# Running sums of the Mamba decays made once a layer as rows, and their differences taken by VectorE, in a hybrid mLSTM and Mamba-2 decoder trunk

## The chip, the cores and the metric

The kernel runs on 1 core of one Trainium2 chip. The metric is the device time of one execution in microseconds. The runs shown are medians; a profiled execution gives the span, which runs from its first to its last instruction.

## The reference

Two layers of a decoder trunk on 256 tokens of width 1024, all in float32: a half-step SwiGLU, a mixer with an mLSTM branch and a Mamba-2 branch, a second half-step SwiGLU, and a gated per-layer input embedding. The change concerns the Mamba-2 branch. It has 32 heads of width 64 in 4 groups, a state of 128, and chunks of 128 tokens, so two chunks. What matters of it:

```python
acs = jnp.cumsum((dt * a_neg).reshape(bsz, nc, L, ng, ne), axis=2)      # running sums of the decays
ah = jnp.transpose(acs, (0, 1, 3, 4, 2))
decay = jnp.exp(jnp.where(causal, ah[..., :, None] - ah[..., None, :], -jnp.inf))
cb = jnp.einsum('bctgn,bcsgn->bcgts', cc, bc)
y_intra = jnp.einsum('bcgts,bcgets,bcsgep->bctgep', cb, decay, xw)
w_end = jnp.exp(ah[..., -1:] - ah)                                     # state handed to chunk 1
y_inter = jnp.einsum('bctgn,bcgepn->bctgep', cc, s_start) * jnp.exp(acs)[..., None]
```

For each head and chunk a 128x128 matrix exp(acs[t] - acs[s]) for t >= s is wanted, and for chunk 1 also exp(acs[t], from the chunk's start).

## The kernel before

**Precision.** A float32 operand x is split into x_hi (rounded to the matmul's fast type) and x_lo = x - x_hi. A projection is three matmuls: hi by hi, hi by lo, lo by hi.

**Stages.** A layer is an FFN, the mixer (a loop over 4 groups, the second to fourth in a hardware loop), the second gate, the merge of the branches, the output projection, a second FFN and the embedding gate. A weight tile (a unit, 1 MB) goes through a ring of three buffers: SyncE loads it, ScalarE writes w_hi (`hi`, L524), VectorE writes w_lo (`lo`, L911), and TensorE uses it in 48 matmuls of 256 columns (L1521). In the mixer `step(p)` on both engines means: make the copy of the unit that comes two places after place p, counted from 0. Every engine has its order written out by hand and waits on semaphores.

**One group's units on TensorE.** In groups 1 to 3: BC, QK, X01, X23, V, Z0, Z1, O, GA; in group 0 V comes first. `feat(..., between=f)` runs f in the middle of a unit (or, with place=0, after its first half). Between the units stand the products of the mixer. `cb` multiplies C by B into bank 5, `scores` makes the mLSTM's scores, `chunk_heads` (L1776) applies them and needs btok, a copy that ScalarE makes after VectorE's `mask_cb`. `inputs_transposed` (L1786) gives VectorE the inputs in token order, `state` (L1798) needs xwe from VectorE, and `outputs` (L1809) needs the decays times cb.

**Decays.** For each head, ScalarE makes R = tri_le scaled by the head's decay column, hi and lo (`part_of`, L637, one 128x128 instruction per head and part). TensorE's `segments(c, half)` multiplies tri_gt by R of four heads (two matmuls of 512 columns, L1744 and L1745) and gets acs[t] - acs[s] above the diagonal and 0 below; ScalarE's `decay(c)` exponentiates (L667). `from_start` does the same with a matrix of ones for chunk 1 (L1751, L1752), and `decay_from_start` exponentiates it into cs (L677). R of chunk 0 for the next group is built late in the group before; R of chunk 1 is built between the two exponentials of `decay(0)`.

**VectorE in groups 1 to 3, in order.** Evacuate BC; convolution of BC (`conv(0)`, L1146 and L1149); queries and keys; `step(1)`; `silu(0)` (L1160), which needs ScalarE's `tanh_conv(0)` (L662); `step(2)`; `distances` (L1176); `step(3)`; evacuate X01; `conv(1)`; `silu(1)`; `weigh_scores` (L1188), which needs GpSimd's masked exponential of `score_exp`; evacuate X23; `conv(2)`; `silu(2)`; `mask_cb` (L1182); `step(4)`; evacuate Z0; `step(5)`; weighted inputs (L1207, L1211); the gates, `step(6)`, `step(7)`, the heads' norm, `step(8)`, the outputs (L1337 to L1354) and `step(9)`.

**ScalarE in groups 1 to 3, in order.** `step(1)`, `decay(0)`, `tanh_conv(0)`, `step(2)`, `step(3)`, `decay(1)`, `tanh_conv(1)`, `score_exp`, `step(4)`, and so on. In group 0 the order is `decay(0)`, the token columns, `step(5)`, `decay(1)`, `tanh_conv(0)`, `score_exp`, `decay_from_start`, `step(6)`, `tanh_conv(1)`.

Of the kernel before, what the change touches and what calls it, by code (L numbers as in the profile page):

```python
# [5 lines left out]
F32 = mybir.dt.float32  # L6
# [6 lines left out]
P = 128  # L13
# [10 lines left out]
def trunk(nc, T, out):  # L24
# [53 lines left out]
    with ctx:  # L78
# [25 lines left out]
        tri_gt_r = sb("tri_gt_r", [P, P], F32R)  # L104
        dA_hi = sb("dA_hi", [P, NC, SH], F32R)
# [6 lines left out]
        top[0] = place(feat_at, 512, 1024)  # L112
        ha_hi = sb("ha_hi", [P, 2 * MH, S], F32R)
        ha_lo = sb("ha_lo", [P, 2 * MH, S], F32R)
        top[0] = place(top[0], 512, 1024)
# [5 lines left out]
        m_lo = sb("m_lo", [P, KD, S], F32R)  # L121
        y_feat = sb("y_feat", [P, SI // P, S])
# [9 lines left out]
        ones_r = sb("ones_r", [P, P], F32R)  # L132
# [13 lines left out]
        dA_lo = sb("dA_lo", [P, NC, SH], F32R)  # L146
# [40 lines left out]
        xwe_at = late + NC * EH * HP * 4  # L187
# [10 lines left out]
        zth_at = a  # L198
        zth, a = at("zth", [P, 2, S], F32, a)
        R_hi = [at(f"R_hi{b}", [P, 4, P], F32R, off)[0] for b, off in enumerate((xwe_at, zth_at))]  # L200
        R_lo = [at(f"R_lo{b}", [P, 4, P], F32R, late + b * 4 * P * 4)[0] for b in range(2)]
# [62 lines left out]
        def rows(x):  # L264
# [4 lines left out]
        names = """up0_done h1T_done res_done uT_done gate_done y_out_ready rB_ready z_tanh o_tanh gate_tanh evac v_ready par_ready rdiag_ready rB_done ydiag_ready yB_done yB_ready wsm_hi_ready wsm_ready pre_row_ready pre_ready acs_exp cs_ready y_done ysum_ready  # L269
# [3 lines left out]
            dA_ready dA_split ea_ready cum_done cum_exp row_tr row_ready row_back tok_ready r_built seg_done exp_done  # L273
# [133 lines left out]
        def _(pool):  # L407
# [42 lines left out]
            def group(lay, g, first, last):  # L450
# [18 lines left out]
                if not first:  # L469
                    pool.wait_ge(sem["cbm_done"], G + 1)  # L470
                    for c in range(NC):
                        pool.wait_ge(sem["exp_done"], G * 4 + (2 * c + 2))
# [3 lines left out]
                    pool.wait_ge(sem["acs_exp"], G * 2 + 2)  # L476
# [9 lines left out]
            for lay in range(DEPTH):  # L486
                row_norm(lay * 4)
                row_norm(lay * 4 + 1)
                g_.memset(M4[:, :, :], 0.0).then_inc(sem["m4_clear"], 1)
                group(lay, 0, True, False)  # L490
# [13 lines left out]
        def _(act):  # L504
# [125 lines left out]
            def groups(lay):  # L630
                def body(g, first, last):
                    G = act.snap(lay * NG + g)

                    def part_of(dst, part, g, c, half):

                        for e in range(4):
                            i = a_.activation(dst[half][:, e, :], tri_le[:, :], ACT.Copy,  # L637
                                              scale=part[:, c, bass.ds(g * EH + (4 * half + e), 1)].bitcast(F32))
                        return i

                    def distances_of(g, c, half):
                        part_of(R_hi, dA_hi, g, c, half)
                        part_of(R_lo, dA_lo, g, c, half).then_inc(sem["r_built"], 1)
# [29 lines left out]
                    def decay_from_start():  # L673

                        for b in range(2):
                            act.wait_ge(sem["seg_done"], G * 6 + (5 + b))
                            a_.activation(cs[:, 4 * b:4 * b + 4, :], bank[6 + b][:, :].rearrange("p (e t) -> p e t", e=4),  # L677
                                          ACT.Exp).then_inc(sem["acs_exp"], 1)
# [11 lines left out]
                    if first:  # L690
# [13 lines left out]
                        act.wait_ge(sem["dA_split"], lay + 1)  # L704
# [4 lines left out]
                        a_.activation(w_end[:, :], bank[7][:, 0:SH], ACT.Exp).then_inc(sem["cum_exp"], 1)  # L709
# [6 lines left out]
                        decay(0)  # L716
# [13 lines left out]
                    else:  # L730
# [9 lines left out]
                        decay_from_start()  # L740
# [49 lines left out]
                    if not last:  # L790
                        act.wait_ge(sem["yi_done"], G + 1)
                        act.wait_ge(sem["zth_ready"], G * 2 + 2)
                        for half in range(2):
                            part_of(R_hi, dA_hi, g + 1, 0, half)
                        act.wait_ge(sem["y_done"], G + 1)
                        for half in range(2):
                            part_of(R_lo, dA_lo, g + 1, 0, half).then_inc(sem["r_built"], 1)
# [1219 lines left out]
```

## Time and profile before

| | us |
|---|---|
| median of 3 runs (1563.87 to 1566.05) | 1564.98 |
| the profiled execution's own time | 1564.03 |
| its span | 1562.3 |
| busy in the span: TensorE / VectorE / ScalarE / GpSimd | 1538.5 / 1073.3 / 808.3 / 150.2 |

The mixer's groups of layer 0 lie between 204 and 465 us of the span, those of layer 1 some 769 us later. In the profile PE is TensorE's matmuls, PEld its weight loads, DVE VectorE, ACT ScalarE, POOL GpSimd; L911 is line 911 of the kernel before. A timeline row has the start, the duration, the engine, line and operation, the tiles (out<-in), how many were merged (x8) and, in brackets, how long the engine had been idle and what released it. Matmuls overlap, so the distance between two starts is what one costs.

### The profile page before, as it was taken

To read this page: it belongs to the slowest core of one execution; us is meant where nothing else is said; L and a number is where in the kernel's file an instruction comes from. 1 tells how busy PE (TensorE), PEld (TensorE's weight loads), DVE (VectorE), ACT (ScalarE), POOL (GpSimd) and SP (SyncE) were. 2 spreads that over 40 slices of the span, in tenths; PEclk is the share of its full clock that TensorE was granted. 3 is DMA by queue.
4 is the path that set the end of the run, shared out by engine and by line. 5 is a ranking of instruction groups with operands and counts; after the bars stand their busy time and mean duration, and the time that the engine had idled before them with its cause. 6 is when DMAs were issued, how large, how long until landed. Compare 5 with 4: busy or idle time off the path is not lost.

```text
span 1562.3 us, 28127 instructions
## 1 busy us (share of the span) xinstructions
PE 1538.5 (98%) x11594; PEld 1439.9 (92%) x11594; DVE 1073.3 (69%) x1313; ACT 808.3 (52%) x1141; POOL 150.2 (10%) x144
## 2 busy tenths in 40 slices
PE   7999999999999999999999999999999999999997
PEld 6999999999999979999899999998999999799996
DVE  5556578889887546565665556799889865565555
ACT  6444385664655354343564435755766643543344
POOL 1000011233130000000000000113243000000000
PEclk9999999999999999999999999999999999999999
DMA  8655544456455556655565655445545456465551
GB/s 252 196 198 190 176 156 110 146 153 185 135 159 190 190 167 210 195 188 189 173 191 194 194 194 162 128 143 144 180 134 161 161 190 213 153 207 189 188 189 68
DMA packets 245089, 271.09 MB, mean 174 GB/s; under 512 B 12560, under 2 KB 226152, under 8 KB 245012
## 3 DMA queue, kind: packets, MB, share of 16 engines
q1 hardware_dynamic: 239504, 266.90, 53.7%
q10 hardware_dynamic: 5364, 2.98, 0.7%
q8 instruction: 53, 0.87, 0.2%
q14 instruction: 24, 0.20, 0.0%
q0 software_dynamic: 144, 0.15, 0.0%
HBM read 268.94 MB, written 1.05 MB: 173 GB/s over the span
## 4 chain that ended last, share of the span: by engine, by line
PE 89%; DVE 4%; issue 4%; ACT 2%; DMA 1%; SPq 0%; POOL 0%; ACTq 0%; DVEq 0%; POOLq 0%
PE bank L1521 29%; PE bank L1605 28%; PE bank L1551 8%; PE bank L1552 7%; PE bank L1553 7%; PE bank L1954 1%; PE bank L1809 1%; PE bank L1546 1%; DVE w_lo L911 1%; PE bank L1537 1%; PE bank L1539 1%; PE bank L1538 1%; ACT w_hi L524 1%; DMA w_raw<-in_w_ffn_dram 1%; DVE xcv L1149 1%
## 5 line engine op out<-in xcount | busy, mean ns | idle before, releaser
L911 DVE TENSOR_TENSOR w_lo<-w_raw,w_hi 128x2048 fp32r<-128x2048 f32 x248 | 577.0, 2328 | 315.8 <-ACT w_hi L524 315.5
L524 ACT ACTIVATE w_hi<-w_raw 128x2048 fp32r<-128x2048 f32 x248 | 474.1, 1916 | 307.5 <-PE bank L1605 131.0
L1605 PE MATMUL bank<-f_lo,w_hi 128*128 128x256 f32 x1280 | 355.7, 278 | 0.0
L1605 PE MATMUL bank<-f_hi,w_lo 128*128 128x256 f32 x1280 | 353.5, 276 | 0.0
L1605 PE MATMUL bank<-f_hi,w_hi 128*128 128x256 f32 x1240 | 342.7, 276 | 0.0
L1521 PE MATMUL bank<-u_hi,w_hi 128*128 128x256 f32 x1152 | 326.5, 283 | 1.3 <-DVE w_lo L911 1.3
L1521 PE MATMUL bank<-u_lo,w_hi 128*128 128x256 f32 x1152 | 319.8, 278 | 0.0
L1521 PE MATMUL bank<-u_hi,w_lo 128*128 128x256 f32 x1152 | 319.8, 278 | 0.0
L1605 PEld LDWEIGHTS bank<-f_hi,w_lo 128*128 128x128 f32 x1280 | 240.5, 188 | 0.0
L1605 PEld LDWEIGHTS bank<-f_lo,w_hi 128*128 128x128 f32 x1280 | 240.4, 188 | 0.0
L1605 PEld LDWEIGHTS bank<-f_hi,w_hi 128*128 128x128 f32 x1240 | 232.8, 188 | 0.0
L1521 PEld LDWEIGHTS bank<-u_hi,w_hi 128*128 128x128 f32 x1152 | 216.4, 188 | 6.3 <-issue 4.1
L1521 PEld LDWEIGHTS bank<-u_lo,w_hi 128*128 128x128 f32 x1152 | 216.7, 188 | 1.3
L1521 PEld LDWEIGHTS bank<-u_hi,w_lo 128*128 128x128 f32 x1152 | 217.2, 189 | 0.0
L1551 PE MATMUL bank<-w_hi,h_hi 128*128 128x512 f32 x352 | 137.5, 391 | 0.0
L1553 PE MATMUL bank<-w_hi,h_lo 128*128 128x512 f32 x352 | 137.2, 390 | 0.0
L1552 PE MATMUL bank<-w_lo,h_hi 128*128 128x512 f32 x352 | 137.2, 390 | 0.0
L436 POOL TENSOR_TENSOR rms<-var,m_half 128x2 f32<-128x2 f32 x11 | 7.7, 696 | 1019.9 <-DVE var L947 998.9
L584 ACT ACTIVATE sa<-h1f 128x512 f32<-128x512 f32 x40 | 25.3, 632 | 118.4 <-DVE h1f L995 118.4
L1553 PEld LDWEIGHTS bank<-w_hi,h_lo 128*128 128x128 f32 x352 | 66.1, 188 | 14.0
L1552 PEld LDWEIGHTS bank<-w_lo,h_hi 128*128 128x128 f32 x352 | 66.1, 188 | 12.3
L1551 PEld LDWEIGHTS bank<-w_hi,h_hi 128*128 128x128 f32 x352 | 66.1, 188 | 12.3
(301 smaller groups left out, 2450.8 us busy)
## 6 DMA issues: line engine op xcount, KB each, us to landing
w_raw<-in_w_ffn_dram SPq DMA_DIRECT2D x262, 512.0 KB, 4.4
w_raw<-in_w_in_dram SPq DMA_DIRECT2D x160, 512.0 KB, 4.9
w_raw<-in_w_branch_b_dram SPq DMA_DIRECT2D x32, 512.0 KB, 4.5
w_raw<-in_w_branch_a_dram SPq DMA_DIRECT2D x16, 512.0 KB, 4.5
w_raw<-in_w_out_dram SPq DMA_DIRECT2D x16, 512.0 KB, 4.0
w_raw<-in_w_ple_gate_dram SPq DMA_DIRECT2D x16, 512.0 KB, 4.4
y_feat<-in_w_ple_dram ACTq DMA_DIRECT2D x2, 1024.0 KB, 5.0
h<-in_x_dram SPq DMA_DIRECT2D x2, 512.0 KB, 5.7
```

Source lines behind the costliest of these rows:

```text
L524: a_.activation(whi[slot][:, :, :], raw[slot][:, :, :], ACT.Copy).then_inc(sem["w_hi"], 1)
L584: a_.activation(sa[:, :, :], h1f[:, :, :], ACT.Silu).then_inc(sem["g_silu"], 1)
L911: v_.tensor_tensor(wlo[slot][:, :, :], raw[slot][:, :, :], whi[slot][:, :, :].bitcast(F32), ALU.subtract).then_inc(sem["w_lo"], 1)
L1149: ins = v_.scalar_tensor_tensor(out=dst[:, q, :], in0=src, scalar=gcw[:, j, t:t + 1], in1=dst[:, q, :], op0=ALU.mult, op1=ALU.add)
L1521: i = mm(o, w[slot][:, k, cs], x[:, k, :], start=(k + q == 0 and not seeded), stop=(k == KD - 1 and q == 2 and not seeded), skip_group_che ...
L1537: mm(o, xh[:, k, cs], whi[slot][:, k, :], start=(k == 0), stop=False)
L1538: mm(o, xh[:, k, cs], wlo[slot][:, k, :], start=False, stop=False)
L1539: i = mm(o, xl[:, k, cs], whi[slot][:, k, :], start=False, stop=(k == KD - 1))
L1551: mm(o, xh, wh, start=start, stop=False, skip_group_check=True)
L1552: mm(o, xh, wl, start=False, stop=False, skip_group_check=True)
L1553: return mm(o, xl, wh, start=False, stop=stop, skip_group_check=True)
L1605: i = mm(o, four(w[slot])[:, k, cs], x[:, rows0 + k, :], start=opens, stop=(not start and k == 3 and q == 2), skip_group_check=True)
```

## The change

The decays' running sums are computed once a layer. dA is split into `twin[0]` (hi) and `twin[1]` (lo), each with its 8 heads of a group at columns 0 to 7 and again at 32 to 39. TensorE multiplies the twins by tri_le (16 matmuls of 128 columns), so the sums stand as rows 0 to 7 and 32 to 39. ScalarE rounds them into `acs`, and VectorE replaces rows 32 to 39 by the rest, so that row e plus row 32+e is the full sum. In a group one matmul per head, with a matrix `pick` that has ones in rows e and 32+e, spreads a head's sums over all partitions for both chunks (256 columns). VectorE subtracts the sum at s (`acol`, a column per head and chunk) and clamps at 0; ScalarE exponentiates. Nothing of R is left. The core of the diff (tile placement, semaphore names and unchanged lines left out):

```diff
@@ gpsimd, once a layer, ahead of group 0
+                g_.memset(acs[:, :, :].bitcast(F32), 0.0)
+                for b in range(2):
+                    i = g_.memset(twin[b][:, :, :, :].bitcast(F32), 0.0)
+                i.then_inc(sem["twin_clear"], 1)
+                for b in range(2):
...
+                    i = g_.tensor_tensor(pick[b][:, :, :], ident[:, e].unsqueeze(2).broadcast_to([P, EH // 2, P]),
+                                         ident[:, f].unsqueeze(2).broadcast_to([P, EH // 2, P]), ALU.add)
+                i.then_inc(sem["pick_ready"], 1)
@@ scalar
-                    def part_of(dst, part, g, c, half):
-                        for e in range(4):
-                            i = a_.activation(dst[half][:, e, :], tri_le[:, :], ACT.Copy,
-                                              scale=part[:, c, bass.ds(g * EH + (4 * half + e), 1)].bitcast(F32))
-                        return i
+                    def sums_high():
+                        act.wait_ge(sem["acs_done"], lay + 1)
+                        for b in range(2):
+                            i = a_.activation(acs[0:40, 2 * b:2 * b + 2, :],
+                                              bank[4 + b][0:40, :].rearrange("p (g s) -> p g s", g=2), ACT.Copy)
+                        i.then_inc(sem["acs_hi"], 1)
...
-                    def decay(c):
-                        for b in range(2):
-                            act.wait_ge(sem["seg_done"], G * 6 + (2 * c + b + 1))
-                            a_.activation(seg[:, c, 4 * b:4 * b + 4, :],
-                                          bank[4 + 2 * c + b][:, :].rearrange("p (e t) -> p e t", e=4),
-                                          ACT.Exp).then_inc(sem["exp_done"], 1)
-                            if c == 0:
-                                distances_of(g, 1, b)
...
+                    def decay(half):
+                        act.wait_ge(sem["gap_ready"], G * 2 + (half + 1))
+                        for e in range(4 * half, 4 * half + 4, 2):
+                            a_.activation(cs[:, e:e + 2, :], two(4 + e // 2)[:, :, P:2 * P], ACT.Exp)
+                        a_.activation(seg[:, :, 4 * half:4 * half + 4, :], seg[:, :, 4 * half:4 * half + 4, :],
+                                      ACT.Exp).then_inc(sem["exp_done"], 1)
@@ scalar, group 0
-                        distances_of(g, 0, 0)
-                        distances_of(g, 0, 1)
+                        sums_high()
                         step(3)
...
                         step(5)
+                        act.wait_ge(sem["cum_exp"], lay + 1)
+                        tanh_conv(0, bcv[:, :, :])
+                        decay(0)
+                        score_exp()
                         decay(1)
-                        tanh_conv(0, bcv[:, :, :])
-                        score_exp()
-                        decay_from_start()
                         step(6)
@@ vector
+                    def gaps(half):
+                        dve.wait_ge(sem["cum_exp"], lay + 1)
+                        dve.wait_ge(sem["seg_done"], G * 2 + (half + 1))
+                        for e in range(4 * half, 4 * half + 4):
+                            for c in range(NC):
+                                i = v_.tensor_scalar(seg[:, c, e, :], bank[4 + e // 2][:, (e % 2) * S + c * P:(e % 2) * S + (c + 1) * P],
+                                                     acol[:, c, bass.ds(g * EH + e, 1)], 0.0, ALU.subtract, ALU.min)
+                        i.then_inc(sem["gap_ready"], 1)
@@ vector, group 0
                         conv(1, 1, (2, 3), xcv[:, 0:2, :])
+                        gaps(0)
                         weigh_scores()
+                        evac(X23, xin[:, 0, :, 3:])
+                        gaps(1)
                         mask_cb()
-                        evac(X23, xin[:, 0, :, 3:])
                         silu(1, xcv[:, 0:2, :])
@@ vector, groups 1 to 3
                         step(1)
+                        gaps(0)
                         silu(0, bcv[:, :, :])
                         step(2)
                         distances()
                         step(3)
+                        gaps(1)
                         evac(X01, xin[:, 1, :, 3:])
@@ tensor, once a layer (in gates)
+                pe.wait_ge(sem["dA_split"], lay + 1)
+                for g in range(NG):
+                    for c in range(NC):
+                        o = bank[4 + g // 2][0:40, (g % 2) * S + c * P:(g % 2) * S + (c + 1) * P]
+                        mm(o, twin[0][:, c, g, :], tri_le_r[:, :], start=True, stop=False)
+                        i = mm(o, twin[1][:, c, g, :], tri_le_r[:, :], start=False, stop=True)
+                i.then_inc(sem["acs_done"], 1)
@@ tensor, in a group, in place of segments and from_start
+                    def sums(half):
...
+                        for e in range(4):
+                            i = mm(bank[4 + 2 * half + e // 2][:, (e % 2) * S:(e % 2 + 1) * S], pick[half][:, e, :],
+                                   acs[:, bass.ds(g, 1), :].rearrange("p a b -> p (a b)"), start=True, stop=True)
+                        i.then_inc(sem["seg_done"], 1)
```

In groups 1 to 3 `sums(0)` stands in the middle of QK and `sums(1)` in the middle of X01; in group 0 they stand after `scores` and in the middle of Z0. `cb` now waits for the first `decay`, `inputs_transposed` for the second. VectorE splits dA into the twins in two copies and two subtractions instead of one each, and `sums_low`, two subtractions on 8 partitions, follows `gate_rows` in group 0. A second product next to the one for w_end, 64 columns wide, gives `acol`, which ScalarE copies.

## Rows read from the trace of the kernel before

**Rows 1.** The page: busy time of each engine, its share of the span, instructions.

```profile
PE 1538.5 (98%) x11594; PEld 1439.9 (92%) x11594; DVE 1073.3 (69%) x1313; ACT 808.3 (52%) x1141; POOL 150.2 (10%) x144
```

**Rows 2.** Stretches; length, then busy PE, PEld, DVE, ACT, POOL; clock, DMA share, GB/s.

```profile
281.71:341.96 60.25, 58.30 (x503) 55.58 (x501) 51.95 (x72) 38.29 (x70) 19.73 (x17) 1.00 0.48 140
341.96:403.25 61.29, 61.29 (x529) 59.23 (x528) 53.09 (x74) 38.78 (x70) 19.88 (x16) 1.00 0.53 154
```

**Rows 3.** Timeline, VectorE, groups 2 and 3; start, duration, then [idle before <- releaser].

```profile
340.37 2.29 DVE L911 TENSOR_TENSOR w_lo<-w_raw,w_hi 128x2048 fp32r<-128x2048 f32 x1 [2.59 <-ACT w_hi L524]
...
343.30 0.74 DVE L1146 TENSOR_SCALAR bcv<-xin,gcw,gcb 128x256 f32<-128x256 f32 x2
...
349.57 0.68 DVE L1160 SCALAR_TENSOR_TENSOR bcv<-cth,bcv 128x512 f32<-128x512 f32 x1
350.74 2.29 DVE L911 TENSOR_TENSOR w_lo<-w_raw,w_hi 128x2048 fp32r<-128x2048 f32 x1 [0.49 <-ACT w_hi L524]
...
404.20 0.74 DVE L1146 TENSOR_SCALAR bcv<-xin,gcw,gcb 128x256 f32<-128x256 f32 x2
...
412.03 2.29 DVE L911 TENSOR_TENSOR w_lo<-w_raw,w_hi 128x2048 fp32r<-128x2048 f32 x1 [0.87 <-ACT w_hi L524]
```

**Rows 4.** Timeline, ScalarE, around and in group 2.

```profile
336.23 1.05 ACT L801 ACTIVATE zs<-y_feat 128x1024 f32 x1
...
342.62 0.60 ACT L667 ACTIVATE seg<-bank 128x512 f32<-128x512 f32 x1 [0.49 <-PE bank L1745]
...
348.28 0.61 ACT L662 ACTIVATE cth<-bcv 128x512 f32<-128x512 f32 x1
348.80 3.70 ACT L524 ACTIVATE w_hi<-w_raw 128x2048 fp32r<-128x2048 f32 x2
...
368.53 0.27 ACT L688 ACTIVATE btok<-bank 128x128 f32<-128x128 f32 x1
...
373.35 0.36 ACT L750 ACTIVATE cst<-bank 128x257 f32<-128x257 f32 x1
373.61 0.38 ACT L751 ACTIVATE num<-bank 128x257 f32<-128x257 f32 x1
```

**Rows 5.** Timeline, TensorE, groups 2 and 3.

```profile
341.96 0.39 PE L1744 MATMUL bank<-R_hi,tri_gt_r 128*128 128x512 f32 x1
...
342.42 0.28 PE L1521 MATMUL bank<-u_hi,w_hi 128*128 128x256 f32 x1
342.54 0.28 PE L1521 MATMUL bank<-u_lo,w_hi 128*128 128x256 f32 x1
...
370.06 0.59 PE L1776 MATMUL bank<-vtok,ktok 128*128 128x257 f32 x2
...
371.36 1.03 PE L1786 MATMUL bank<-ident,xcv 128*128 128x128 f32 x8
...
431.34 0.59 PE L1776 MATMUL bank<-vtok,ktok 128*128 128x257 f32 x2
```

**Rows 6.** Groups of ScalarE instructions by line: count, busy us, mean ns, idle before.

```profile
L637 ACT ACTIVATE R_hi<-tri_le,dA_hi 128x128 fp32r<-128x128 f32 x128 | 40.0, 389 | 2.1 <-DVE dA_lo L1086 2.1
```

**Rows 7.** Timeline, VectorE, a burst of eight 128x128 instructions that read PSUM.

```profile
201.76 2.15 DVE L954 SCALAR_TENSOR_TENSOR u_lo<-bank,par,u_hi 128x128 fp32r<-128x128 f32 x8
```

**Rows 8.** Timeline, VectorE and TensorE, group 0 of layer 0.

```profile
238.79 0.69 DVE L1160 SCALAR_TENSOR_TENSOR bcv<-cth,bcv 128x512 f32<-128x512 f32 x1 [5.43 <-ACT cth L662]
...
247.21 0.68 DVE L1160 SCALAR_TENSOR_TENSOR xcv<-cth,xcv 128x512 f32<-128x512 f32 x1
...
243.15 0.60 PE L1760 MATMUL bank<-bcv 128*128 128x128 f32 x4
```

**Rows 9.** Timeline, TensorE, start of the execution.

```profile
10.39 0.63 PE L1552 MATMUL bank<-w_lo,f_hi 128*128 128x512 f32 x1
10.81 0.63 PE L1553 MATMUL bank<-w_hi,f_lo 128*128 128x512 f32 x1
...
18.27 0.39 PE L1552 MATMUL bank<-w_lo,f_hi 128*128 128x512 f32 x1
```

More of the change, by code:

```diff
@@ L103, in trunk @@
         gate_a = sb("gate_a", [P, KD, S])
[L104 to L105 removed]
+        tri_le_r = sb("tri_le_r", [P, P], F32R)
+        acol = sb("acol", [P, NC, SH])
         e_a = sb("e_a", [P, SH])
@@ L112, in trunk @@
         top[0] = place(feat_at, 512, 1024)
+        ha_hi_at = top[0]
         ha_hi = sb("ha_hi", [P, 2 * MH, S], F32R)
+        ha_lo_at = top[0]
         ha_lo = sb("ha_lo", [P, 2 * MH, S], F32R)
+        last_group = 2 * (MH - 1) * S * 4
+        pick = [at(f"pick{b}", [P, EH // 2, P], F32R, off + last_group)[0] for b, off in enumerate((ha_hi_at, ha_lo_at))]
         top[0] = place(top[0], 512, 1024)
@@ L186, in trunk @@
         late = a
-        xwe_at = late + NC * EH * HP * 4
+        twin = [at(f"twin{b}", [P, NC, NG, 40], F32R, late + b * 40 * NC * NG * 4)[0] for b in range(2)]
         xw, a = at("xw", [P, NC, EH * HP], F32, a)
@@ L789, in body @@
                         step(9)
[L790 to L797, printed above, removed]
                     act.wait_ge(sem["ha32_ready"], G + 1)
@@ L1265, in body @@
                         gate_rows(lay)
+                        sums_low(lay)
                         step(3)
@@ L1739, in unit @@
                         kind((K_MIX + p) % RING, p % RING, u_hi, u_lo)
-                    def segments(c, half):
-                        pe.wait_ge(sem["r_built"], G * 4 + (2 * c + half + 1))
-                        mm(bank[4 + 2 * c + half][:, :], tri_gt_r[:, :], R_hi[half][:, :, :], start=True, stop=False)
-                        mm(bank[4 + 2 * c + half][:, :], tri_gt_r[:, :], R_lo[half][:, :, :], start=False, stop=True)\
-                            .then_inc(sem["seg_done"], 1)
-                    def from_start():
-                        for half in range(2):
-                            pe.wait_ge(sem["exp_done"], G * 4 + (3 + half))
-                            mm(bank[6 + half][:, :], ones_r[:, :], R_hi[half][:, :, :], start=True, stop=False)
-                            mm(bank[6 + half][:, :], ones_r[:, :], R_lo[half][:, :, :], start=False, stop=True)\
-                                .then_inc(sem["seg_done"], 1)
+                    def sums(half):
+                        if first:
+                            pe.wait_ge(sem["acs_ready"], lay + 1)
+                            pe.wait_ge(sem["pick_ready"], lay + 1)
+                            pe.wait_ge(sem["cum_exp"], lay + 1)
+                        elif half == 0:
+                            pe.wait_ge(sem["st_ready"], G)
+                            pe.wait_ge(sem["num1_ready"], G)
+                        else:
+                            pe.wait_ge(sem["y_ready"], G)
+                        for e in range(4):
+                            i = mm(bank[4 + 2 * half + e // 2][:, (e % 2) * S:(e % 2 + 1) * S], pick[half][:, e, :],
+                                   acs[:, bass.ds(g, 1), :].rearrange("p a b -> p (a b)"), start=True, stop=True)
+                        i.then_inc(sem["seg_done"], 1)
                     def cb():
                         pe.wait_ge(sem["cv_ready"], G * 3 + 1)
-                        pe.wait_ge(sem["exp_done"], G * 4 + 2)
+                        pe.wait_ge(sem["exp_done"], G * 2 + 1)
                         for c in range(NC):
@@ L1839, in body @@
                         pe.wait_ge(sem["tok_ready"], lay * 2 + 2)
-                        segments(1, 0)
-                        segments(1, 1)
-                        unit(Z0, lambda *a: feat(*a, between=from_start))
+                        sums(0)
+                        unit(Z0, lambda *a: feat(*a, between=lambda: sums(1)))
                         cb()
@@ L1858, in body @@
                         unit(BC, feat)
-                        unit(QK, lambda *a: feat(*a, between=lambda: segments(0, 0)))
-                        segments(0, 1)
-                        unit(X01, lambda *a: feat(*a, between=lambda: segments(1, 0)))
-                        segments(1, 1)
+                        unit(QK, lambda *a: feat(*a, between=lambda: sums(0)))
+                        unit(X01, lambda *a: feat(*a, between=lambda: sums(1)))
                         evac(QK)
@@ L1865, in body @@
                         unit(X23, feat)
-                        unit(V, lambda *a: tok(*a, between=from_start))
+                        unit(V, tok)
                         cb()
```

64 lines of the change are left out of this document (32 added, 32 removed).

## The prediction

> **What bounds the kernel now.** I read the page first: TensorE is busy 98% of the span, VectorE 69%, ScalarE 52%, GpSimd 10% [rows 1]. Nearly all TensorE time is projections that the change leaves alone, so matmuls taken away should shorten the run, if the engines that feed TensorE can follow a faster one. The share of 69% doesn't settle that. In the stretch of one group (layer 0, group 2) VectorE is busy 53.1 of 61.3 us [rows 2], against 69% of the whole, so I went through that stretch instruction by instruction.
>
> VectorE stands still 8.2 us in that group, and the question is whether any of it waits for TensorE. The timelines say that nearly none does. Its largest idle piece (2.59 us) waits for ScalarE's copy of a weight tile, which itself followed a tanh of what VectorE had just written; the others are pieces under 1 us of the same kind, such as the tanh that ScalarE can start only when VectorE's convolution ends. These are round trips that VectorE starts, and no faster TensorE shortens them. The only waiting for TensorE that reaches this loop is ScalarE's 0.49 us before its first exponential of the group, handed on as the 0.49 us that VectorE waits at 350.74 [rows 3, 4]. From group 2 to group 3 VectorE's round takes 404.20 - 343.30 = 60.9 us; without the 0.49 it takes 60.4. TensorE's round is 431.34 - 370.06 = 61.3 us [rows 5]. So two loops are within 0.9 us of each other. In group 1 VectorE's is the longer: TensorE is busy only 58.3 of 60.3 us there [rows 2]. That is the ground of the forecast: a change that takes from TensorE and gives to VectorE's round makes the kernel slower.
>
> **TensorE.** Two 512-column matmuls take from 341.96 to 342.42, 0.23 us each; a 256-column one takes 0.12 us [rows 5]. A group loses 12 of 512 (8 in `segments`, 4 in `from_start`), 2.8 us, and gains 8 of 256, 0.95 us: 1.85 us less, 14.8 us over 8 groups. Once a layer come 16 matmuls of 128 columns on the twins. The nearest row is that of eight transposes of this width, 1.03 us with a last one of 0.27, so 0.11 us from start to start [rows 5]; I take that, 1.8 us, and 0.2 us for the wider sum for `acol`; bounds 0.5 and 4 us a layer. TensorE's own sum is then 14.8 - 4.0 = 10.8 us less, if nothing makes it wait.
>
> **ScalarE.** 256 copies of 128x128 that build R go, 40 us busy for R_hi and as much for R_lo [rows 6], 32 per group. That gives nothing by itself: they fill ScalarE between 342.6 and 348.3, and what VectorE then lacks is the 0.49 us above. The others, late in a group, lie under VectorE's own work (ScalarE still waits for it after them). Six exponentials of 512 from PSUM become four of 256 (start to start 0.26 us [rows 4]) and two of 1024 from SBUF (1.05 us [rows 4]).
>
> **VectorE, groups 1 to 3.** Added are 16 `tensor_scalar` of 128x128 from PSUM. Eight of nearly this kind take 2.15 us in a burst [rows 7]: 2.1 us for each half, 4.2 us a group. Bounds for one: 0.14 us (half of the burst's 0.27) to 0.34 us (the duration of one that is not overlapped, as 8 by 0.34 instead of 2.1): 2.2 to 5.5 us a group. `gaps(0)` stands between `step(1)` and `silu(0)`, and `decay(0)` stands on ScalarE ahead of `tanh_conv(0)`. So where the tanh had long been ready (VectorE starts `silu(0)` at 349.57 without waiting, tanh from 348.28 [rows 3, 4]), this now runs in series, in times of group 2:
> - `gaps(0)` 349.57 to 351.7;
> - `decay(0)` two cs exponentials 0.26 + 0.26, then 1024 elements: the tanh starts at 353.3 and ends 353.9; VectorE has waited 2.3 us;
> - `silu(0)` 353.95 to 354.55;
> - the copy for `step(2)` follows the tanh, 353.8 to 355.7 (1.9 us, [rows 4]); VectorE waits 1.2 us more, and starts at 355.75 instead of 350.74: +5.0.
>
> `gaps(1)` then adds 2.1 us ahead of the evacuation of X01. Its ScalarE part (1.6 us) is hidden under convolution 1 (3.5 us). So `mask_cb`, `step(4)` and all behind them come 7.1 us later. The waits for nothing but round trips further down the group remain; none of them is for an engine that runs ahead, so none absorbs the delay. Group 3 had a longer wait for that copy, 0.87 us at 412.03 [rows 3]: +6.7. Group 1 has the same order and waits of its own: +7.0.
>
> TensorE has no room for this: its chunk_heads at 370.06 waits for btok, ready at 368.80 [rows 4, 5]. There it will stand: a new round is 60.4 + 7.0 = 67.4 us, against 59.4 us of TensorE work, so 8 us of waiting a group, mostly before chunk_heads and some before V's weights.
>
> **Group 0.** Walked in the same way from layer 0. ScalarE's `sums_high` waits for the sums of the twins, which TensorE ends near 225.9 (its small gate products start at 223.0) behind X01's first half, and VectorE's `sums_low` adds 1.3 us; but VectorE stood 5.43 us before `silu(0)` [rows 8] and this covers it: `silu(0)` comes at 238.0 instead of 238.79. Then: `step(4)` 239.1, conv(1) to 245.1, `gaps(0)` to 247.2. Now `weigh_scores` needs `score_exp`, which stands behind `decay(0)` (to 248.85), then 0.4 us of exp and 0.95 us on GpSimd: 250.2, 3 us idle. Evacuation of X23, `gaps(1)` to 253.3, and `silu(1)` waits for tanh(1), behind `decay(1)` (1.6) and `step(6)` (1.8) on ScalarE: 257.3 instead of 247.21 [rows 8], +10.1; 0.2 of it is lost in the wait for the transposed inputs. TensorE meets it twice: `cb`, at 243.15 before [rows 8], waits for `decay(0)` until 248.9, and chunk_heads for btok. If ScalarE could reach `step(6)` earlier, as it would with a shorter pair of exponentials, +7; if the twins' sums come later than I put them, +12.
>
> The new memsets, `pick` on GpSimd (once a layer, about 5 us) and the double split of dA (0.2 us) run at the front of the layer: GpSimd is busy a tenth of the span [rows 1], and its taps are first used by the convolution of group 0, over 10 us later. I cost them at 0; without that cover up to 2 us a layer. No DMA is added or moved.
>
> **Sum.** A layer: 9.9 + 7.0 + 7.1 + 6.7 = 30.7 us, less the room that TensorE had: between 0 and the 1.26 us from btok to chunk_heads; I take 0.6: 30.1. Behind the groups TensorE is the bound again and gives nothing back. The profiled execution took 1564.0 us; 1564.0 + 60.2 = 1624.2. The median of the runs is 0.95 us over that execution: **1625 us**. The 10.8 us that TensorE saves don't count, since they become waiting. Its own range, 2.2 to 5.5 us for the 16 instructions and 7 to 12 for group 0: 1608 to 1639.
>
> **Rivals.**
> - *Waits hidden, work not* (12%). ScalarE, without its copies, would be ready early enough that only VectorE's 4.2 us a group remain, against 0.9 us of room. For it speaks ScalarE's idle time; against it, that `decay(0)` itself starts only after `gaps(0)`. 8 x (4.2 - 0.4) = 30: 1595 us.
> - *TensorE stays the bound* (8%, the other side). If `silu(0)` and the weight splits had over 7 us of room in each group, the 10.8 us would come through, and with them up to 2 us of group 1's waits a layer (60.25 - 58.30 [rows 2]): 1550 us. The place is X23's and Z1's weights, which VectorE finishes at 349.66 and 370.4, under 2 us ahead of use by my reading of TensorE's order; it decides below 0.9 us of net delay a group. TensorE's 98% speaks for it, and rows 3 against it.
> - *The clock falls* (8%). The granted clock is 1.00 in all stretches read [rows 2], and TensorE never stands long there. At the start of the run, after standing, matmuls of 512 columns come every 0.42 us, not 0.23 (1.2 instead of 2.4 GHz), at 10.39 and still shortly before 18.27 [rows 9]. Should each long stop (one or more a group, 5 to 6 us) bring back such a stretch, its 7.9 us of half speed cost 3.9 us, of which some 1.5 lie under VectorE's lag: 8 x 2.4 = 19 us more, 1644 us. The Trainium skill (TensorE: Matmul & The Clock Gate, "HAM oscillation — how this bites in real kernels") has the mechanism: a loop in which TensorE stands waiting each turn restarts at the throttled clock. By that rule this rival would be the likeliest. No row before shows a fall in mid-run, so I leave it at 8%.
> - *No change* (3%): losses meet gains of the same size.
>
> **How the numbers follow.** Forecast 69%. Faster is the second rival, 8%; within 0.2% (3 us, what a measurement tells from none) 3%; slower 89%. The range reaches below to the waits-hidden rival and above nearly to the clock's: 1594 to 1646.
>
> **What would show it.** Right: VectorE waits about 2.3 us before `silu(0)` for ScalarE's tanh and about 1.2 us for the copy behind it; eight-bursts of 2.1 us; the round of a group 67 to 68 us in groups 1 to 3; TensorE's idle before chunk_heads, with btok as releaser, about 6 us; in group 0, `cb` waits for an exponential. Wrong: TensorE busy over 99% of the groups and a round near 59.5 us, or bursts of well under 2 us. If the granted clock falls below 1.00 within the groups, the third rival is in it.

## The result, and the profile after the change

The changed kernel takes 1625.79 us (1625.22 to 1628.05, 4 runs) against 1564.42 us (1563.60 to 1566.05, 4 runs) beside it: ratio 1.0395 [1.0383, 1.0407], slower. Its profiled execution has a span of 1624.0 us (before 1562.3).

The page's busy line, against [rows 1]: TensorE fell from 98% to 95%, and ScalarE lost 72 us of work without any gain. TensorE's busy time rose by 11.4 us though it was given less work; the mean granted clock of its execution fell from 0.998 to 0.982.

```profile
PE 1549.9 (95%) x11598; PEld 1450.3 (89%) x11598; DVE 1109.3 (68%) x1448; ACT 736.6 (45%) x891; POOL 153.2 (9%) x154
```

One round of VectorE (group 2's first convolution to group 3's) by stretches, as in [rows 2]: length, busy PE, PEld, DVE, ACT, POOL, then clock. It has grown from 60.9 to 67.9 us, TensorE is no longer busy all through it, and its clock is below 1.00.

```profile
360.33:428.26 67.93, 61.87 (x519) 59.49 (x519) 56.92 (x90) 29.42 (x37) 19.51 (x15) 0.95 0.47 139
```

VectorE's timeline in group 2, which answers to [rows 3]. Both bursts of eight and both predicted waits are there: 2.19 us before `silu(0)`, 1.11 us before `step(2)`'s w_lo.

```profile
366.59 2.15 DVE L1215 TENSOR_SCALAR seg<-bank,acol 128x128 f32<-128x128 f32 x8
370.93 0.69 DVE L1165 SCALAR_TENSOR_TENSOR bcv<-cth,bcv 128x512 f32<-128x512 f32 x1 [2.19 <-ACT cth L669]
372.73 2.29 DVE L902 TENSOR_TENSOR w_lo<-w_raw,w_hi 128x2048 fp32r<-128x2048 f32 x1 [1.11 <-ACT w_hi L534]
...
377.66 2.16 DVE L1215 TENSOR_SCALAR seg<-bank,acol 128x128 f32<-128x128 f32 x8
379.73 0.68 DVE L1140 TENSOR_TENSOR xin<-bank,rB 128x512 f32<-128x512 f32 x1
```

ScalarE beside it ([rows 4] before). It stood idle 9.61 us, then did the exponentials, the tanh and two weight copies in a row, with VectorE waiting for the third and fourth link.

```profile
368.78 0.66 ACT L675 ACTIVATE cs<-bank 128x256 f32<-128x256 f32 x2 [9.61 <-DVE seg L1215]
369.32 1.06 ACT L676 ACTIVATE seg<-seg 128x1024 f32<-128x1024 f32 x1
370.27 0.63 ACT L669 ACTIVATE cth<-bcv 128x512 f32<-128x512 f32 x1
370.79 3.72 ACT L534 ACTIVATE w_hi<-w_raw 128x2048 fp32r<-128x2048 f32 x2
```

TensorE's chunk_heads, where [rows 5] had no stop: it waits 5.83 us for btok. Behind the stop, a pair of 257-column products takes 0.85 us (393.94 to 394.79), half speed: at full clock such a pair took some 0.43 us (258.49 to 258.93 in e_order).

```profile
392.95 1.20 PE L1806 MATMUL bank<-vtok,ktok 128*128 128x257 f32 x2 [5.83 <-ACT btok L687]
393.94 1.06 PE L1807 MATMUL bank<-vtok,scT 128*128 128x257 f32 x2
394.79 1.07 PE L1808 MATMUL bank<-vtok,scT 128*128 128x257 f32 x2
```

The same place by stretches: the granted clock, 1.00 all through the groups of before [rows 2], is 0.71 in the mean after the stop and 1.00 again in the next stretch. Layer 0 has five such falls, one with each of TensorE's stops of over 2 us: one of 5.78 us ahead of cb in group 0, one of 2.56 us early in group 1, and those of 4.29, 5.83 and 5.59 us ahead of chunk_heads in groups 1 to 3.

```profile
386.00:393.00 7.00, 1.17 (x11) 1.01 (x10) 6.16 (x13) 2.75 (x7) 0.62 (x1) 0.80 0.00 0
393.00:400.00 7.00, 7.00 (x38) 6.34 (x39) 7.00 (x5) 4.63 (x5) 7.00 (x2) 0.71 0.59 151
400.00:407.00 7.00, 7.00 (x60) 6.01 (x60) 6.88 (x5) 1.91 (x1) 3.87 (x2) 1.00 0.55 148
```

Group 0 on VectorE, against [rows 8]: `silu(0)` waits 2.40 us in place of 5.43, `weigh_scores` waits for GpSimd, `silu(1)` for ScalarE.

```profile
238.94 0.69 DVE L1165 SCALAR_TENSOR_TENSOR bcv<-cth,bcv 128x512 f32<-128x512 f32 x1 [2.40 <-ACT cth L669]
...
250.59 0.42 DVE L1193 TENSOR_TENSOR scT<-pm,bank 128x256 f32<-128x256 f32 x1 [2.77 <-POOL pm L467]
...
257.67 0.69 DVE L1165 SCALAR_TENSOR_TENSOR xcv<-cth,xcv 128x512 f32<-128x512 f32 x1 [3.66 <-ACT cth L669]
```

### The profile page after: what moved, and what is told of

The parts are those of the page before. It is cut to its first block, busy times and chain, and to the rows that moved or that the text cites. A ratio compares the mean times of both kernels' runs of the same rounds, so it can differ in the third digit from the quotient of the medians.

```text
span 1624.0 us, 27967 instructions
## 1 busy us (share of the span) xinstructions
PE 1549.9 (95%) x11598; PEld 1450.3 (89%) x11598; DVE 1109.3 (68%) x1448; ACT 736.6 (45%) x891; POOL 153.2 (9%) x154
## 4 chain that ended last, share of the span: by engine, by line
PE 69%; DVE 12%; issue 10%; POOL 4%; ACT 4%; DMA 1%; DVEq 0%; SPq 0%; ACTq 0%; POOLq 0%; another core or an unknown queue 0%
PE bank L1623 26%; PE bank L1539 16%; PE bank L1569 7%; PE bank L1570 7%; PE bank L1571 7%; DVE w_lo L902 2%; POOL seg L474 2%; DVE xcv L1154 2%; ACT w_hi L534 2%; DVE seg L1215 2%; PE bank L1979 1%; PE bank L1564 1%; POOL cs L477 1%; DVE xin L1140 1%; DVE xcv L1151 1%
```

## The experiments

Theory from here on: VectorE's chain, with the round trips it makes through ScalarE, sets the length of a group; it grew by its own 4.2 us and by two waits that ScalarE's order makes. All times are medians; all ratios are to the kernel before, which ran beside each. All kernels are the changed kernel with an edit, but for e_before9, which is the kernel before with one.

| kernel | what is different | us | ratio | VectorE's round, groups 2 to 3 |
|---|---|---|---|---|
| e_gaps2 | 8 more instructions on VectorE a group | 1642.33 | 1.0497 [1.0480, 1.0515] | 70.0 |
| e_pe4 | 24 more products on TensorE a group | 1626.18 | 1.0393 [1.0376, 1.0410] | 67.9 |
| e_fill | idle products in TensorE's stop, groups 1 to 3 | 1622.66 | 1.0371 [1.0355, 1.0387] | 67.9 |
| e_wide | 4 wide instructions for 8 narrow ones | 1616.06 | 1.0331 [1.0315, 1.0347] | 67.0 |
| e_order | ScalarE: tanh and copies ahead of exponentials | 1603.89 | 1.0255 [1.0238, 1.0272] | 64.7 |
| e_order0 | e_order, and `gaps(0)` earlier in group 0 | 1602.39 | 1.0247 [1.0232, 1.0263] | 64.7 |
| e_ofill | e_order, and idle products in group 0's stop | 1600.03 | 1.0225 [1.0210, 1.0241] | 64.7 |
| e_order00 | e_order0, and chunk_heads' copies earlier in group 0 | 1595.10 | 1.0196 [1.0180, 1.0212] | 64.7 |
| e_before9 | kernel before, weight copy of `step(9)` earlier | 1571.51 | 1.0043 [1.0027, 1.0058] | 63.2 |
| e_relu | the differences on ScalarE | 1557.79 | 0.9958 [0.9942, 0.9975] | 60.3 |
| e_relu9 | e_relu, weight copy of `step(9)` earlier | 1554.75 | 0.9936 [0.9923, 0.9950] | 59.6 |
| e_relu9s | e_relu9, its subtraction on VectorE earlier | 1554.26 | 0.9934 [0.9921, 0.9948] | 59.6 |

**Which engine sets the round: e_gaps2 and e_pe4.** One adds work to VectorE, the other to TensorE.

```diff
@@ e_gaps2, in gaps(0)
+                            for n in range(8):
+                                v_.tensor_scalar(cs[:, n, :], ...)
@@ e_pe4, in sums
-                        for e in range(4):
+                        for e in [*range(4)] * 4:
```

> The changed kernel with eight more tensor_scalar of 128x128 from PSUM in gaps(0) of every group, written to cs ahead of the exponentials that fill it, so that nothing of the result changes. Theory (VectorE and its round trips are the bound): 8 x 2.1 = 17 us more than the changed kernel, 1643 us. Rival (VectorE's work is hidden under TensorE and only waits count): within 3 us of 1626.

> The changed kernel with every product of sums made four times over, 24 more matmuls of 256 columns a group, 2.8 us of TensorE, more than the 1.85 us that the change took from it. Theory (TensorE stands about 8 us a group): the time stays at 1626 within 3 us. Rival (TensorE is the bound in the groups): 8 x 2.8 = 22 us more, 1648 us.

Eight more instructions a group cost 16.5 us, which over the 8 groups is 8 x 2.07, their bare length; 24 more products a group, at 0.12 us some 2.9 us of TensorE, cost 0.4 us, inside the spread (1623.64 to 1628.53). In groups 1 to 3 TensorE has room and VectorE none.

**Where the two waits come from: e_order.** The same work in another order on ScalarE.

```diff
@@ groups 1 to 3
                         step(1)
-                        decay(0)
                         tanh_conv(0, bcv[:, :, :])
                         step(2)
+                        decay(0)
                         step(3)
@@ group 0
                         tanh_conv(0, bcv[:, :, :])
-                        decay(0)
                         score_exp()
+                        decay(0)
+                        tanh_conv(1, xcv[:, 0:2, :])
                         decay(1)
                         step(6)
-                        tanh_conv(1, xcv[:, 0:2, :])
```

> The changed kernel, with ScalarE's order alone changed: in groups 1 to 3 tanh_conv(0) and the copy of step(2) stand ahead of decay(0), in group 0 score_exp stands ahead of decay(0), and tanh_conv(1) ahead of decay(1). VectorE's work is the same. Theory (the 61 us are VectorE's 4.2 us of gaps a group plus the waits that decay(0) puts before silu(0) and step(2)): in groups 1 to 3 the 2.2 us before silu(0) and nearly all of the 1.1 us before step(2) go, about 3.1 us a group; in group 0 about 5 us. 1626 - 2 x (3 x 3.1 + 5) = 1597 us. Rival (only the added work counts, the waits would come elsewhere): within 3 us of 1626.

VectorE in group 2: no wait before `silu(0)`, 0.16 us in place of 1.11 before the copy. The round lost 3.2 us.

```profile
361.80 2.15 DVE L1215 TENSOR_SCALAR seg<-bank,acol 128x128 f32<-128x128 f32 x8
363.87 0.68 DVE L1165 SCALAR_TENSOR_TENSOR bcv<-cth,bcv 128x512 f32<-128x512 f32 x1
...
367.43 2.29 DVE L902 TENSOR_TENSOR w_lo<-w_raw,w_hi 128x2048 fp32r<-128x2048 f32 x1 [0.16 <-ACT w_hi L534]
```

The kernel took 1603.9 us against 1597 expected. The miss is in group 0, which was to gain 5 us a layer. VectorE reached `silu(1)` 6.6 us earlier (251.06), but then waited for TensorE (group 0 from first convolution to first convolution: 59.1 to 58.2 us). Its rows, TensorE's cb and VectorE's next wait:

```profile
249.06 1.20 PE L1790 MATMUL bank<-bcv 128*128 128x128 f32 x4 [6.21 <-ACT seg L676]
```

```profile
265.89 1.29 DVE L1222 TENSOR_TENSOR xw<-bank,spx 128x512 f32<-128x512 f32 x2 [4.96 <-PE bank L1816]
```

**What held group 0: e_order0, e_order00, e_ofill.** Each starts from e_order. e_order0 takes `gaps(0)` earlier, to free the banks that cb wants. e_order00 takes the copies that chunk_heads wants earlier too. e_ofill leaves the stop and fills it with products nobody reads.

```diff
@@ e_order0, vector, group 0
                         silu(0, bcv[:, :, :])
+                        gaps(0)
                         distances()
...
                         conv(1, 1, (2, 3), xcv[:, 0:2, :])
-                        gaps(0)
@@ e_order00, besides: vector, group 0
+                        mask_cb()
                         weigh_scores()
...
-                        mask_cb()
@@ e_order00, scalar, group 0
                         tanh_conv(1, xcv[:, 0:2, :])
+                        transposed_copies()
                         decay(1)
                         step(6)
-                        transposed_copies()
@@ e_ofill, tensor, group 0, ahead of cb
+                        evac(X01)
+                        for _ in range(21):
+                            mm(bank[order.index(Z1) % RING][:, :], zeros[:, :], ...)
```

> The kernel with tanh and weight copies ahead of the exponentials on ScalarE (1603.9 us), and in group 0 VectorE's gaps(0) moved from behind conv(1) to ahead of distances. Group 0 of that kernel gained only 1.5 us instead of 5. Theory (there TensorE's stop ahead of cb, 6.21 us until the banks of sums(0) are read, took the lead over ScalarE's order): gaps(0) runs 5 to 6 us earlier, cb starts near 243.5 us instead of 249.06, no stretch at half clock behind it, and the transposed inputs come 5 us earlier: 1594 us (1590 to 1599). Rival (something else holds group 0, as weights or the units' banks): cb earlier, the time 1603 +- 2 us.

> The kernel with VectorE's gaps(0) moved ahead in group 0 (1602.4 us), whose cb started 6 us earlier (243.02 us) while chunk_heads then stood until 253.90 us, behind ScalarE's copy of btok (253.51 us), itself behind decay(1) and the weight copy of step 6. Here group 0 masks cb ahead of weigh_scores on VectorE and copies ktok and btok ahead of decay(1) on ScalarE. Theory (one stop of TensorE had only taken the place of the other): chunk_heads at about 249.5 us without a stop and without the stretch at half clock, the transposed inputs then wait for silu(2) at 258 us instead of 262.6 us, 3.4 us less a layer: 1595 us (1592 to 1598). Rival (group 0 is held elsewhere): 1602 +- 2 us.

> The kernel with tanh and weight copies ahead of the exponentials on ScalarE (1603.9 us), and in group 0 21 products of 512 columns that nobody reads put into TensorE's stop of 6.21 us ahead of cb. In that kernel TensorE is busy without a stop from cb (249.06 us) to the transposed inputs, for which VectorE waits 4.96 us, and its first products come 0.214 us apart (granted clock 0.52 from 249 to 255 us) instead of 0.117. Theory (where TensorE leads, the fall of the clock is paid in full): 20 products at 0.097 us and 0.6 us of cb less, 2.5 us a layer: 1599 us (1597 to 1601). Rival (the fall costs nothing here either): 1604 +- 1 us.

e_order0 came out by its rival: cb started 6 us earlier, and then chunk_heads stood 4.52 us in its place (the trace calls it "issue"; chunk_heads starts just behind ScalarE's copy of btok, 253.51 + 0.29).

```profile
243.02 0.68 PE L1790 MATMUL bank<-bcv 128*128 128x128 f32 x4 [0.50 <-ACT seg L676]
...
253.90 1.11 PE L1806 MATMUL bank<-vtok,ktok 128*128 128x257 f32 x2 [4.52 <-issue]
```

e_order00 removed that one as well, and group 0 fell to 52.6 us, near the 52.0 of before; 1595.1 us, as expected. So with the waits gone, and only VectorE's added work left, the kernel is 31 us over the kernel before, where the prediction's first rival had put work without waits: 8 x (4.2 - 0.4) = 30.

```profile
242.49 0.68 PE L1790 MATMUL bank<-bcv 128*128 128x128 f32 x4 [0.50 <-ACT seg L676]
248.89 0.59 PE L1806 MATMUL bank<-vtok,ktok 128*128 128x257 f32 x2
```

e_ofill prices the clock. These are the same 6 us after the stop, first e_order, then e_ofill:

```profile
249.00:255.00 6.00, 5.94 (x29) 5.97 (x30) 5.52 (x11) 4.26 (x7) 0.00 (x0) 0.52 0.02 4
```

```profile
249.00:255.00 6.00, 5.73 (x49) 5.76 (x50) 5.96 (x13) 4.47 (x8) 0.00 (x0) 1.00 0.05 6
```

With 0.52 of the clock TensorE did 29 products, with 1.00 it did 49. Group 0 became some 2.5 us shorter in both layers (58.17 to 55.60, 57.92 to 55.39), the kernel 3.9 us. The missing 1.2 us lie between the layers: from group 3's first convolution to group 0's of the next layer 600.3 us became 601.4, which no run explains.

**The clock in the changed kernel: e_fill.** The same filling ahead of chunk_heads in groups 1 to 3 of the changed kernel.

```diff
                         unit(Z0, feat)
+                        evac(X23)
+                        for _ in range(22):
+                            mm(bank[order.index(Z1) % RING][:, :], zeros[:, :], ...)
                         chunk_heads()
```

> The changed kernel, with 22 products of 512 columns that nobody reads put into TensorE's stop of some 6 us ahead of chunk_heads in groups 1 to 3 (4.8 us of work at full clock), so that its granted clock doesn't fall to 1.2 GHz behind the stop. Theory (the fall is there, but lies in the lag of TensorE behind VectorE's chain): the granted clock behind chunk_heads stays at 1.00, the time stays 1626 us (1623 to 1628). Rival (the fall is part of the loss): each stretch of 3.4 to 6.8 us at half clock gives back 1.7 to 3.4 us, in 6 groups 10 to 20 us: 1606 to 1616 us.

The clock stayed at 1.00 behind the filled stops (compare the same stretch of the changed kernel above), and the rounds did not move at all: 68.9 and 67.9 us as in the changed kernel.

```profile
393.00:400.00 7.00, 7.00 (x61) 6.79 (x59) 6.88 (x6) 3.78 (x6) 7.00 (x2) 1.00 0.71 180
```

The kernel gained 3.1 us, slightly past the theory's bound and far from the rival's 10 to 20. The two profiled executions lie 2.6 us apart: 1.0 us of it stands ahead of the mixer, where the kernels are the same, and 1.9 us behind the last groups, where TensorE leads again. There VectorE's wait for it shrinks from 2.28 to 0.84 us (changed kernel first, then e_fill); in the second layer from 1.77 to 0.81.

```profile
505.28 0.69 DVE L1434 TENSOR_TENSOR gate_b<-bank,rB 128x512 f32<-128x512 f32 x1 [2.28 <-PE bank L1539]
```

```profile
502.88 0.69 DVE L1434 TENSOR_TENSOR gate_b<-bank,rB 128x512 f32<-128x512 f32 x1 [0.84 <-PE bank L1539]
```

Two falls of the clock a layer are left in e_fill, those of group 0 and of early group 1 (at 245.1 and 306.5 us). What they cost in the changed kernel no run tests.

**The price of one small instruction: e_wide.** This kernel leaves out chunk 1's own column, so its decays of chunk 1 are other numbers; it is there for the time alone.

```diff
-                            for c in range(NC):
-                                i = v_.tensor_scalar(seg[:, c, e, :], ...)
+                            i = v_.tensor_scalar(seg[:, :, e, :], ..., acol[:, 0, ...], 0.0, ALU.subtract, ALU.min)
```

> The changed kernel with the clamped differences of each half in 4 instructions of 128x256 in place of 8 of 128x128; chunk 1's differences are taken with chunk 0's column, so its decays are others. Theory (VectorE's round is the bound and a part of each small instruction is fixed cost; 128x256 rows of other operations take 0.41 us alone, about 0.34 each back to back): 4 x 0.34 + 0.07 = 1.4 us instead of 2.15 per half, 1.5 us less a group, 12 us over both layers: 1614 us (1610 to 1618). Rival (cost goes by elements alone): 1625 +- 2 us.

Half the instructions with the same elements take 1.65 us, not 2.15:

```profile
362.89 1.65 DVE L1214 TENSOR_SCALAR seg<-bank,acol 128x256 f32<-128x256 f32 x4
```

From start to start that is 0.39 us for 256 columns and 0.26 for 128: 0.13 us for each 128 columns and as much fixed. So half the cost of these bursts was their number. The kernel gained 9.7 us, of 12 expected.

**The differences on ScalarE: e_relu.**

```diff
@@ scalar, in decay(half), in place of VectorE's gaps
+                        for e in range(4 * half, 4 * half + 4):
+                            for c in range(NC):
+                                i = a_.activation(seg[:, c, e, :], bank[4 + e // 2][...],
+                                                  ACT.Relu, scale=-1.0, bias=acol[:, c, bass.ds(g * EH + e, 1)])
...
-                                      ACT.Exp).then_inc(sem["exp_done"], 1)
+                                      ACT.Exp, scale=-1.0).then_inc(sem["exp_done"], 1)
@@ scalar, group 0
+                        tanh_conv(1, xcv[:, 0:2, :])
                         step(6)
-                        tanh_conv(1, xcv[:, 0:2, :])
```

> The changed kernel with gaps moved from VectorE to ScalarE: 16 instructions Relu(acol - sums) of 128x128 a group, inside decay, whose exponential then has scale -1; in group 0 tanh_conv(1) stands ahead of step(6). VectorE gets nothing new, TensorE keeps its saving. Theory: VectorE's round is again about 60.4 us, TensorE's 59.4, so 0.9 us less a group than before in groups 1 to 3 and some 1 us in group 0: 1557 us (1552 to 1563). Rival (ScalarE's chain of 8 Relu, 2 and 1 exponentials, about 3.8 us ahead of tanh_conv(0), delays silu(0) as gaps did): above 1570 us.

ScalarE in group 2: eight Relu in 2.18 us, as fast as VectorE's burst, and done in time that was idle. All of VectorE's loss is gone: its round is 60.3 us, against 60.9 before the change. In group 0 the moved tanh has a share in the gain that no run sets apart; groups 1 to 3 have no other change than the differences.

```profile
341.31 2.18 ACT L676 ACTIVATE seg<-bank,acol 128x128 f32<-128x128 f32 x8 [0.77 <-PE bank L1773]
343.33 0.70 ACT L680 ACTIVATE cs<-bank 128x256 f32<-128x256 f32 x2
343.86 1.12 ACT L682 ACTIVATE seg<-seg 128x1024 f32<-128x1024 f32 x1
345.22 0.63 ACT L669 ACTIVATE cth<-bcv 128x512 f32<-128x512 f32 x1 [0.24 <-DVE bcv L1160]
```

**VectorE's last wait: e_relu9, e_relu9s, e_before9.** The 2.59 us that VectorE waits for `step(9)`'s copy [rows 3], taken out by an earlier copy on ScalarE, in e_relu and in the kernel before.

```diff
@@ e_relu9, from e_relu, and e_before9, from before: scalar
-                    if first:
-                        step(9)
+                    step(9)
...
-                        step(9)
@@ e_relu9s, besides: vector
-                    evac(GA, gate_a[:, bass.ds(g * 2, 2), :])
                     if not first:
                         step(9)
+                    evac(GA, gate_a[:, bass.ds(g * 2, 2), :])
```

> The kernel with the clamped differences on ScalarE (1557.8 us), and in groups 1 to 3 the weight copy of step 9 on ScalarE moved ahead of the copy into ha_hi, for which VectorE waits 2.59 us at the end of each group. Theory (VectorE's chain of work and waits is what sets the round): VectorE's round falls from 60.3 to about 57.8 us, so that TensorE's own work (59.4 us) sets it: 1.4 us less in each of 3 groups of 2 layers, 1549 us (1546 to 1553), and VectorE's wait moves to another place of the group. Rival (the round of 60.3 us is already TensorE's): 1558 +- 1 us, with the wait of 2.59 us turned up elsewhere in full.

> The kernel before, with the weight copy of step 9 of groups 1 to 3 on ScalarE moved to behind the tanh of unit O, ahead of the copies into R_hi. It takes out the wait of 2.59 us on VectorE that my prediction counted in VectorE's natural round of 60.4 us beside TensorE's 61.3. Theory (TensorE sets the round before): nearly nothing, 1562 us (1558 to 1566), with VectorE's wait turned up elsewhere. Rival (VectorE's chain was already the bound before): 2.6 us less in each of 6 groups, 1549 us.

> The kernel with the clamped differences and the early weight copy on ScalarE (1554.8 us), in which VectorE's subtraction into w_lo of step 9 took 4.22 us instead of 2.29, beside GpSimd's addition into ysum (335.36 us, 2.41 us). Here that subtraction stands ahead of evac(GA) on VectorE, so that it starts before the addition. Theory A (two operations on SBUF alone, one of VectorE and one of GpSimd, run one after the other): w_lo takes 2.3 us again and the addition waits. For the time, theory T (the round of 59.6 us is TensorE's own work, 59.4 us): 1554 us (1552.5 to 1555.5). Rival V (the round is still VectorE's): 1.9 us less in each of 6 groups, 1543 us.

e_relu9 gained 3.0 us of some 9 expected. The wait was gone, and VectorE's subtraction took 4.22 us instead of 2.29. GpSimd's and VectorE's rows:

```profile
335.36 2.41 POOL L484 TENSOR_TENSOR ysum<-ysum,zs 128x1024 f32<-128x1024 f32 x1 [8.76 <-ACT zs L797]
335.69 4.22 DVE L906 TENSOR_TENSOR w_lo<-w_raw,w_hi 128x2048 fp32r<-128x2048 f32 x1
337.71 2.25 POOL L457 COPY gdk<-dcol 128x4 f32 x1
```

GpSimd's addition ends at 337.77; 2.29 us of plain work from there would end at 340.06, and the subtraction ends at 339.91. GpSimd's copy of 4 columns (0.27 us in group 1 of the kernel before) then takes 2.25 us, until the subtraction ends. In e_relu9s, with VectorE first, it is the other way round:

```profile
334.97 2.28 DVE L906 TENSOR_TENSOR w_lo<-w_raw,w_hi 128x2048 fp32r<-128x2048 f32 x1
335.24 4.28 POOL L484 TENSOR_TENSOR ysum<-ysum,zs 128x1024 f32<-128x1024 f32 x1 [8.76 <-ACT zs L797]
```

Theory A holds: the two run one after the other. The time hardly moved (0.5 us, not separable), with the round at 59.6 us, so the long subtraction isn't what kept e_relu9 from its 9 us. Theory T holds: 59.6 us is TensorE's own work, so that a round of 60.3 had some 0.8 us to gain, not 1.4; the rounds of groups 1 and 2 in both layers did gain 0.8 each, which makes up the 3 us. TensorE is busy without a break here in e_relu9:

```profile
340.55:400.11 59.56, 59.56 (x523) 58.01 (x522) 54.44 (x73) 33.68 (x53) 19.46 (x15) 1.00 0.54 158
```

e_before9 went against both its theories, 7.4 us slower. The early weight copy stood 2.82 us in ScalarE's queue for its buffer, ahead of the copies that build R and of the one into ha_hi; VectorE's wait moved to ha_hi and grew, and the subtraction then met GpSimd:

```profile
340.31 0.69 DVE L1352 TENSOR_TENSOR ha_lo<-osg,ha_hi 128x512 f32 x1 [4.35 <-ACT ha_hi L798]
...
341.18 2.40 POOL L484 TENSOR_TENSOR ysum<-ysum,zs 128x1024 f32<-128x1024 f32 x1 [12.20 <-ACT zs L800]
...
341.52 4.21 DVE L909 TENSOR_TENSOR w_lo<-w_raw,w_hi 128x2048 fp32r<-128x2048 f32 x1
```

So it doesn't tell whether the 2.59 us were free before. It fits the prediction's reading of VectorE's round: the stretch from y_feat to the next convolution grew by 2.7 us (10.2 to 12.9), and 60.4 + 2.7 = 63.1 us, against a measured round of 63.2, longer than TensorE's 61.3 before.

## Why the prediction was right

- **The bound.** Two loops within 0.9 us of each other, VectorE's fed by round trips: e_gaps2, e_pe4 and e_relu confirm it from three sides.
- **VectorE's steps.** Predicted 2.1 us a burst, waits of 2.3 and 1.2 us; measured 2.15, 2.19, 1.11. The round was to be 67.4 us and is 67.9. The 0.5 us are a slip of the prediction: its +5.0 us already starts at 350.74, behind the wait of 0.49, and for the round this wait was taken off once more; its own steps give 60.9 + 7.0 = 67.9. The sum of the forecast used the steps and is free of the slip. From the first convolution of one group to the next, group 1 grew by 6.9 us (predicted 7.0), group 2 by 7.0 (7.1 less room). e_order shows that 3.2 us of it were ScalarE's order, e_relu that the rest was the bursts.
- **Group 0.** `silu(1)` was to come at 257.3 and came at 257.67; `silu(0)` at 238.0, came at 238.94; cb until 248.9, was 249.60. About 1 us of each is a later start of this execution: w_lo at 205.98 before stands at 207.11 after and at 206.54 in e_order, ahead of anything that the change touches. So group 0 with its front cost about 9.0 us in layer 0, against 9.9. Without the later start the profiled execution grew by 60.6 us, against 60.2 in the sum; that the median came within 0.8 us of the forecast is in part luck, as single terms were off by as much. I had it held by ScalarE alone; e_order showed a second chain right behind (TensorE's stops before cb and chunk_heads), worth over 5 us (58.2 to 52.6), which the sum did not need.
- **Group 3 and the clock.** In layer 0, group 3 and the front and group 0 behind it grew by 16.7 us together, predicted 6.7 + 9.9. The third rival's mechanism, left at 8%, was true and its price wrong: the granted clock falls to 0.71 in the 7 us after group 2's stop. The Trainium skill (TensorE: Matmul & The Clock Gate, "HAM oscillation — how this bites in real kernels") says that a loop in which TensorE stands waiting each turn starts each turn at the throttled clock; the trace agrees, with that 0.71. But filling six of the eight stops that the rival priced gave back 3.1 us, of 14 at its 2.4 us each; VectorE's waits behind the last group account for 1.44 in layer 0 and 0.96 in layer 1. I took 1.5 us of each stretch as hidden; in groups 1 and 2 all of it is. The forecast held because these stretches lie under VectorE's lag, and not because the clock stayed up. The price of group 0's stop in the changed kernel stays open.
- **TensorE.** Its waiting, "about 6 us" before chunk_heads with btok as releaser, is 5.83. The 10.8 us that the change takes from TensorE fit what is gained once VectorE is relieved: e_relu9s is 9.9 us faster than before. As it has the earlier weight copy and another order too, it doesn't measure the 10.8 by themselves.

## What to carry to other kernels

An engine at 69% of a span can be one microsecond from being the bound: read its loop in the stretch, subtract only the idle pieces that wait for the engine you are about to speed up, and what is left is its round. An operation moved between engines costs its length plus what its new queue position makes others wait for; with the differences on VectorE this change cost 61 us, with them on ScalarE, which was idle at that moment, it gained 6.5. When taking one wait away, look at what the freed instruction will then run beside.

## What the runs showed of the hardware

- A subtraction of VectorE and an addition of GpSimd, both with two inputs in SBUF, did not overlap: w_lo takes 4.22 us beside ysum instead of 2.29 (e_relu9), or ysum 4.28 instead of 2.40 (e_relu9s), whichever starts second. The one that waits shows as a long instruction and not as idle time. VectorE's evacuation from PSUM (0.68 us) ran beside ysum at its usual length.
- A stop of 5.8 to 6.2 us of TensorE brought the granted clock down to its 1.2 GHz level (0.52 in the 6 us behind it in e_order; products 0.214 us apart, not 0.117). A stop of 2.56 us in the changed kernel was followed by a fall as well. Filled with idle products, the stops left the clock at 1.00. The cost was nil where TensorE trails another engine (e_fill, groups 1 and 2) and 2.5 us a stop where it leads (e_ofill, group 0).
- A `tensor_scalar` of 128 columns from PSUM costs 0.26 us from start to start (0.39 for 256 columns, so half of it is fixed); ScalarE's Relu with a bias column does the same in 0.25.
